# Gate tables of a product-key expert layer: one 256-column product a token instead of a 128-column float32 one, and gathered rows moved between two layers

## The reference, cut to what matters

```python
vals, flat = lax.top_k(cand, PEER_TOPK)
e1 = jnp.take_along_axis(i1, flat // PEER_TOPK, axis=-1)
e2 = jnp.take_along_axis(i2, flat % PEER_TOPK, axis=-1)
experts = e1 * PEER_NKEYS + e2
gates = jax.nn.softmax(vals, axis=-1)
hid = jax.nn.gelu(jnp.einsum('cd,chkd->chk', xc, u_tab[ec]))      # first layer
out = jnp.einsum('chk,chkd->cd', gc * hid, v_tab[ec])             # second layer
```

## Time and profile before

| | us |
|---|---|
| median of 3 runs | 2308.82 (2307.72 to 2310.43) |
| the profiled execution | 2308.78 |
| its span in the trace | 2307.1 |
| first layer of the experts, units 0 to 127 | 941 to 1640 |
| second layer, units 128 to 255 | 1640 to 2289 |

### The profile page before, as it was taken

The page is one execution under the profiler, slowest core; times in us unless marked ns, Lnnn a source line. Parts: engine busy times, 40 slices in busy tenths (PEclk is TensorE's granted clock), DMA queues, the critical chain, the costliest instruction groups (busy, mean ns, idle before and its releaser), DMA issues.

```text
span 2307.1 us, 35944 instructions
## 1 busy us (share of the span) xinstructions
PE 2272.5 (99%) x13374; PEld 2069.4 (90%) x13374; DVE 1670.8 (72%) x2057; ACT 1220.4 (53%) x1150; POOL 474.9 (21%) x430
## 2 busy tenths in 40 slices
PE   7999999999999999999999999999999999999997
PEld 6888888888888889999999999999999999999997
DVE  5544777666655555888899989897678778878775
ACT  5534555655554344666666566565544444444443
POOL 0001342000000000333456422222222222122100
PEclk9999999999999999999999999999999999999999
DMA  7755556544456656666676899898999999999982
GB/s 281 273 194 212 203 204 214 185 168 171 165 218 221 225 198 233 229 238 237 226 278 245 324 334 336 325 335 315 355 365 357 361 361 364 368 373 366 355 313 87
DMA packets 122285, 623.73 MB, mean 270 GB/s; under 512 B 12000, under 2 KB 40928, under 8 KB 61776
## 3 DMA queue, kind: packets, MB, share of 16 engines
q1 hardware_dynamic: 58752, 423.65, 49.7%
q0 software_dynamic: 25616, 156.65, 18.1%
q10 hardware_dynamic: 37824, 42.18, 5.1%
HBM read 576.29 MB, written 46.14 MB: 270 GB/s over the span
## 4 chain that ended last, share of the span: by engine, by line
PE 90%; DVE 7%; ACT 2%; issue 1%; DMA 1%; DVEq 0%; POOL 0%; ACTq 0%; SPq 0%; POOLq 0%
PE psum L1322 18%; PE psum L1273 16%; PE psum L963 10%; PE psum L965 10%; PE psum L964 10%; PE psum L1323 8%; PE psum L1274 8%; PE psum L1300 2%; DVE w_lo L1410 2%; DVE w_lo L1402 1%; PE psum L1223 1%; PE psum L1224 1%; PE psum L1225 1%; PE psum L1019 1%; ACT w_hi L579 1%
## 5 line engine op out<-in xcount | busy, mean ns | idle before, releaser
L1273 PE MATMUL psum<-h2T,w_hi 128*128 128x448 f32 x2048 | 644.6, 373 | 0.7 <-DVE w_lo L1410 0.4
L1322 PE MATMUL psum<-w_ul,w_hi 128*128 128x448 f32 x2048 | 642.7, 375 | 1.8 <-DVE w_ul L1823 1.8
L1274 PE MATMUL psum<-h2T,w_lo 128*128 128x224 f32 x2048 | 543.4, 265 | 0.0
L1323 PE MATMUL psum<-w_ul,w_lo 128*128 128x224 f32 x2048 | 539.9, 264 | 0.0
L1402 DVE TENSOR_TENSOR w_lo<-w_raw,w_hi 128x2048 fp32r<-128x2048 f32 x144 | 333.0, 2318 | 212.6 <-ACT w_hi L579 211.3
L1322 PEld LDWEIGHTS psum<-w_ul,w_hi 128*128 128x128 f32 x2048 | 384.3, 188 | 31.4 <-issue 2.6
L1273 PEld LDWEIGHTS psum<-h2T,w_hi 128*128 128x128 f32 x2048 | 383.8, 187 | 30.8 <-issue 0.8
L579 ACT ACTIVATE w_hi<-w_raw 128x2048 fp32r<-128x2048 f32 x144 | 275.7, 1915 | 255.7 <-DMA w_raw<-in_w_units 218.9
L1323 PEld LDWEIGHTS psum<-w_ul,w_lo 128*128 128x128 f32 x2048 | 390.9, 191 | 0.0
L1274 PEld LDWEIGHTS psum<-h2T,w_lo 128*128 128x128 f32 x2048 | 390.2, 191 | 0.0
L1410 DVE TENSOR_TENSOR w_lo<-raw_x,w_hi 128x2048 fp32r<-128x2048 f32 x128 | 294.1, 2300 | 77.4 <-ACT w_hi L591 75.8
(11 more groups left out here) (336 smaller groups left out, 2816.1 us busy)
## 6 DMA issues: line engine op xcount, KB each, us to landing
w_raw<-in_w_units SPq DMA_DIRECT2D x272, 1024.0 KB, 5.7
raw_x<-in_w_units SPq DMA_DIRECT2D x128, 1024.0 KB
g_tab<-tab_scratch POOLq DMA_DIRECT2D x32, 896.0 KB, 8.0
h_in<-hid_scratch POOLq DMA_DIRECT2D x64, 448.0 KB
hid_scratch<-hst ACTq DMA_DIRECT2D x32, 448.0 KB, 6.0
tab_scratch<-gate_a ACTq DMA_DIRECT2D x14, 1024.0 KB, 6.9
proj_scratch<-evac ACTq DMA_DIRECT2D x24, 512.0 KB, 4.4
x_nat<-in_x POOLq DMA_DIRECT2D x2, 2048.0 KB, 8.8
```

The costliest lines, as they stand in the source:

```text
L1273: pe.matmul(psum[:, k % 4, 0:2 * NU].rearrange("p (a t) -> p a t", a=2), uh, h2T[:, c, :, G:S], start=c == 0, stop=False, skip_group_check ...
L1274: ins = pe.matmul(psum[:, k % 4, NU:2 * NU], ul, h2T[:, c, 0, G:S], start=False, stop=c == KC - 1, skip_group_check=True)
L1322: pe.matmul(psum[:, c, 0:2 * NU].rearrange("p (a t) -> p a t", a=2), w_hi[:, s, o:o + P], ul, start=first, stop=False, skip_group_check=True)
L1323: return pe.matmul(psum[:, c, 0:NU], w_lo[:, s, o:o + P], ul[:, 0, :], start=False, stop=False, skip_group_check=True)
```

## The change

Constants and slots: a table step becomes half as large (`TH` = 8 tokens, `NHALF` = 28 steps), one after each odd k of i = 8 to 14. `PRE` goes from 32 to 18 gathers in the first layer, 4 of them before i = 8, then after k = 1 and 5; `V_SLOTS` from 32 to 46, mostly k = 1, 3 and 5. The turning of picks goes through bank 2, which the first layer's units use too.

Each half step: DVE compares both key indices in one tensor_tensor of 128x2048 (`picks`); ACT multiplies one comparison by the upper part of the gate (8 activations of 128 columns) while POOL multiplies it by the lower part (`second_lower`, one tensor_tensor of 128x1024); PE makes 8 fp32r products of 256 columns, upper and lower part side by side; ACT copies the lower 1024 columns from PSUM into `low`, DVE adds it to the upper ones into `gate_a` (`table_added`), and ACT stores 1 MB after every second half step.

```diff
-PRE = 32
-PRE_EARLY = 5
+PRE = 18
+PRE_EARLY = 4
+PRE_ROUND = {8: (5,), 9: (1, 5), 10: (1, 5), 11: (1, 5), 12: (1, 5), 13: (1, 5), 14: (1, 5), 15: (1,)}
+PRE_SLOTS = [(4, 7), (5, 7), (6, 7), (7, 3)] + [(i, k) for i in PRE_ROUND for k in PRE_ROUND[i]]
-V_SLOTS = sorted([(0, 5)] + [(i, k) for i in range(1, U_IT - 1) for k in (1, 5)] + [(2, 7), (6, 7), (10, 7)])
+V_SLOTS = sorted([(0, 5), (0, 7), (3, 7), (4, 7), (7, 7)] + [(i, k) for i in range(1, U_IT - 1) for k in (1, 3, 5) if (i, k) != (4, 5)])
...
+            def second_lower(hb):
+
+                pool.wait_ge(picks_done, hb + 1)
+                if hb:
+                    pool.wait_ge(tab_done, hb)
+                pool.tensor_tensor(hot2a[:, :, 1, :], picked[:, 1, :, :].bitcast(F32),
+                                   gate_lo[:, G + hb * TH:G + (hb + 1) * TH, None].to_broadcast([P, TH, PEER_NK]), ALU.mult).then_inc(hot2_done, 1)
...
             for i in range(I_TAB, I_END):
                 for j in range(4):
+                    second_lower((i - I_TAB) * 4 + j)
                     hidden_sum(i * 4 + j, j % 2)
...
+            def table_slot(i, k):
+                hb = 4 * (i - I_TAB) + k // 2
+                if k % 2 == 0:
+                    if 1 <= hb <= NHALF:
+                        act.wait_ge(tab_done, hb)
...
+                        act.activation(low[:, :, :], tables[:, :, 1, :], ACT.Copy).then_inc(low_out, 1)
+                    if hb < NHALF:
+                        act.wait_ge(picks_done, hb + 1)
...
+                        for j in range(TH):
+                            t = G + hb * TH + j
+                            ins = act.activation(hot2a[:, j, 0, :], picked[:, 1, j, :].bitcast(F32), ACT.Copy, scale=gate_hi[:, t:t + 1].bitcast(F32))
+                        ins.then_inc(hot2_done, 1)
...
-            def table(tb):
+            def table(hb):
 
-                pe.wait_ge(hot1_done, tb + 1)
-                pe.wait_ge(hot2_done, tb + 1)
...
+                pe.wait_ge(picks_done, hb + 1)
+                pe.wait_ge(hot2_done, hb * 2 + 2)
...
+                for j in range(TH):
+                    ins = pe.matmul(tables[:, j, :, :], picked[:, 0, j, :], hot2a[:, j, :, :], start=True, stop=True, skip_group_check=True)
                 ins.then_inc(tab_done, 1)
...
+            def picks(hb):
+
+                if hb:
+                    dve.wait_ge(hot2_done, 2 * hb)
+                    dve.wait_ge(tab_done, hb)
+                dve.tensor_tensor(picked[:, :, :, :], iota[:, None, None, :].to_broadcast([P, 2, TH, PEER_NK]),
+                                  rtT[:, 0:2, G + hb * TH:G + (hb + 1) * TH, None].to_broadcast([P, 2, TH, PEER_NK]), ALU.is_equal).then_inc(picks_done, 1)
+
+            def table_added(hb):
+
+                dve.wait_ge(low_out, hb + 1)
+                if hb == 0:
+                    dve.wait_ge(hg_done, 1)
+                elif hb % 2 == 0:
+                    dve.wait_ge(tab_st, 16 * (hb // 2))
+                dve.tensor_tensor(staged[:, hb % 2 * TH:(hb % 2 + 1) * TH, :], tables[:, :, 0, :], low[:, :, :], ALU.add).then_inc(tab_out, 1)
...
-                    if k % 4 == 0 and tables:
-                        tb = i * 2 + (k // 4 - 2 * I_TAB)
...
-                        picks_hot(tb)
+                    hb = 4 * (i - I_TAB) + k // 2
+                    if k % 2 == 0 and tables and hb < NHALF:
...
+                        picks(hb)
                     lo_wide(i * 8 + (U0 + k + AHEAD), k + AHEAD)
+                    if k % 2 == 0 and tables and 1 <= hb <= NHALF:
+                        table_added(hb - 1)
```

160 lines of the change are left out of this document (76 added, 84 removed).

## The result

The changed kernel takes 2316.12 us in the median of 9 executions (2314.2 to 2317.56), beside 2309.55 us (2307.72 to 2311.22, 9 executions) for the kernel before on the same chip. The ratio is 1.0028, with a 95% interval of 1.002 to 1.0036: slower by 0.28%. I had predicted 2300 us, with 2287 to 2315 as the range. The profiled execution has a span of 2315.9 us, that of before 2307.1.

What follows compares the result with a forecast made beforehand. PE, busy 99% of the span, was taken to bound the kernel, with DVE second at 72%. The sum was 2308.8 - 21.3 + 3 + 1.6 + 7.9 = 2300.0 us, range 2287 to 2315.

Steps and rivals of the forecast that it cites:

- Tables on PE: PE's table products: fourteen steps of 50.1 us become 28 half steps of 1.03 us, 28.8 us; PE gains 21.3 us.
- Rival (d): PE's table products: fp32r products of 256 columns take what float32 ones took (0.22 us); 2322 us, chance 0.02.
- the sentence on the table store: Every second addition waits for the 1 MB store, landing after 6.9 us in the median, 21 once; nothing counted.
- 17 us. It has room: ACT's work (splits, evacuations and gelus, copies, small instructions) takes 17 us of the 22.1 of four units.
- the 3 us of the sum: PE's added waits in the first layer's table chain, from DVE and POOL sharing access: 3 us, ends 0 and 17.
- the 17 us at the upper end of that term: Upper end of PE's table-chain waits, if multiplication and handing over cost 0.5 us more each.
- The common access of DVE and POOL: First layer: DVE and POOL hold each other up over SBUF, needing 22.4 us in four units against PE's 22.1.
- behind a DVE split that begins first: Table chain: POOL's multiplication waits for the comparison and such a split; 6.8 us of 10 used, 3 us lag free.
- Rival (b): Closed chain of tables becomes the bound if POOL's multiplication costs 0.6 us more than 2.35; 2326 or 2313 us, chance 0.15.
- First table: PE's wait ahead of the first table, 1.9 us before, becomes about 3.5 us, 1.6 more (0 to 5).
- Second layer: 14 more rows make DVE late and PE wait, mostly around the sums: 7.9 us, ends 0 and 14.
- Transfers: Second layer's 14 more gathers, 14.7 MB, make 385 GB/s where 395 was seen; they fit, barely, and nothing is counted.

Runs made afterwards that it cites:

- e1: Changed kernel with the hidden store issued by SyncE between two loads of weights, no longer by ScalarE: 2331.5 us, ratio 1.0096.
- e15: Kernel before with the new tables alone (32 gathered rows in each layer) and an eighth of each table stored: 2319.1 us, ratio 1.0038.
- e5: Changed kernel with an eighth of each table stored, the second layer reading only the two groups of rows there: 2296.1 us, ratio 0.9944.
- e16: Changed kernel with DVE's work on the second layer's rows cut to an eighth, but for one row, all gathers kept: 2307.8 us, ratio 0.9993.
- e10: Changed kernel with three gathered rows moved from ahead of the second layer's sums to later places: 2319.0 us, ratio 1.004.
- e11: Changed kernel with DVE, in place of GpSimd, making the lower product of the first half step: 2313.1 us, ratio 1.0019.
- e9: Changed kernel with the sum of an even half step written over `low`, and copied to `gate_a` by ACT one unit later: 2331.2 us, ratio 1.009.
- e6: Changed kernel with DVE's addition ahead of the split of the same unit: 2317.1 us, ratio 1.0023, inconclusive.
- e7: As e6, with ACT also issuing the table store ahead of its split: 2314.3 us, ratio 1.0021, inconclusive.
- the kernel with the rows alone: Kernel before with its old tables, and gathered rows placed as in the change (18 and 46): 2311.7 us, ratio 1.0013.
- e13: Changed kernel with the edits of e1 and e9 together, ACT's copy at the end of its unit: 2307.0 us, ratio 0.9991.

## Why the prediction was wrong

- **Tables on PE**: right, and a little low. 23.4 us gained where I had 21.3; a half step takes 0.96 us, not 1.03. Rival (d) is out.
- **The step that failed** is the sentence on the table store: "issued some 9 us before, it lands after 6.9 in the median ... so nothing is counted". I took the landing from the earlier trace rows, where the store has its own place among the transfers. The change issues it in another unit, beside two loads and a hidden store, and it landed after 11.1. In 5 of 13 steps DVE waited for it, 3.0 us in all, and without the hold it would have been far more (e1: 31.1). Nor did I ask what ACT issues next behind it, when I wrote "17 us. It has room". That is the hidden store, some 3 us later where it was 13.1 (1363.26 and 1376.33 in the kernel before), and each such issue held ACT for 1.9 to 4.8 us; that made the addition late in 11 of the 13 steps. Together 16.5 us of waits and 1.6 us of lower clock, for the 3 us of the sum. That the 17 us at the upper end of that term come near is luck: they were there for a dearer multiplication and slower handing over.
- **The common access of DVE and POOL**: the mechanism exists and the sum was near (e15: 24.0 us with two rows, the sum 24.7), but by itself it isn't what ended last: e5 runs at 21.98 with POOL's product whole. One premise of mine failed with the store: that POOL's multiplication stands "behind a DVE split that begins first". Behind a held issue of ACT it began ahead of the split in 8 of 13 steps. What the Trainium skill states in "SBUF — State Buffer", section "Who interferes with whom", that a VectorE instruction with two SBUF inputs contends with a GpSimd instruction that reads SBUF, agrees with the trace here: the split of 2.28 us took up to 3.80 beside the product, or the product of 1.90 us up to 3.9 beside the split. POOL's product took 1.90 us undisturbed, where I had 2.35, and DVE's addition 1.9 to 2.0, within my 1.2 to 2.4. (The lookup of 512 columns in the earlier trace rows has a quarter of the 2048 columns that take 4.65 us, not a third; nothing of the sum hangs on it.)
- **Rival (b)** was the nearest in its result, 2313 to 2326, and had 0.15. Its form (the chain of tables becomes the bound) came true, its price (GpSimd's product in itself) not.
- **First table**: 2.7 us more of waiting where I had 1.6; right in kind. The lower clock behind it, 2.8 us, I had not.
- **Second layer**: 7.6 us measured (674.5 against 666.9), 7.9 predicted, by DVE's rows as said (e16). How it came was half right: behind the sums PE waited 4.1 us where it was 0.7, so 3.4 more where I had 4.1, but 1.0 in four other places where I had 3.8, and 2.7 us of lower clock that I had not. That the total came out is in part luck. Three of the rows in other places (e10) cost as much.
- **Transfers**: right in the second layer (e16: 383 GB/s moved, and its time fell all the same). They were full in another place, behind the table stores (a share of 0.99 in the 10.7 us shown), where a store's landing hung on them.
- **The list of VectorE's instructions before** in the section on the change covers two units, not four: two more splits and one more row belong to the four.

## What to carry to other kernels

When a change moves a store, read from the trace what else is in flight in the new place and what the issuing engine issues next; the landing time of the old place isn't the store's own. With a single staging buffer such a store can stop the chain twice, at its landing and at the next issue of its queue, and here freeing one alone gained nothing: cut the transfer itself first, to see what both are worth. A small delay can also turn round which of two engines goes first where they share an access, and cost more than itself: 0.3 us of it became 1.9 here. The two waits of PE of over 4 us cost some 7 each by the trace, with the lower clock behind them; removing most of the first (e11) gave 3.0 us in the median.

## What the runs showed of the hardware

- An issue on ACT's queue 2.5 to 3.9 us behind a 1 MB store of 512-byte pieces held the engine for 1.9 to 4.8 us in the changed kernel, and one 1.9 to 3.9 us behind it for 4.6 to 6.1 us in e9; 13 us behind it, or behind a store of an eighth (e5), it took 0.34 us. The distance does not settle it alone: in e6 and e7, mostly 3.7 us behind such a store, it took 0.34 to 1.1 us. What else does, no run shows. The Trainium skill, "DMA: Bandwidth & Descriptors", section "Issuing engines are not separate DMA queues", calls the time to initiate a transfer usually small relative to the transfer; here it was not, and it was on the path.
- Where VectorE's split (two inputs in SBUF) began 0.15 us ahead of GpSimd's product, it took 2.28 us and the product 3.88 (e5); where it began 0.25 us behind it, it took 3.80 and the product 1.90 (changed kernel). VectorE's addition with one input in PSUM took 1.93 us there, and at most 2.03 in the whole run.
- The same 1 MB store landed after 5.3 us (medians) in the kernel with the rows alone, 6.9 before, 11.1 in the changed kernel and 12.8 in e13, with other transfers beside it each time.
- The granted clock fell to 0.50 behind waits of PE of 4.1 and 4.6 us, and once behind one of 1.9 us, but behind none of the other twelve of 0.2 to 2.0 us.
